# Expert rows added in DRAM to a residual row per token, in place of pair rows summed at the end

## The reference

```
ids = g_idx[..., None] * EXPERTS_PER_GROUP + e_idx
gates = jnp.sum(jax.nn.one_hot(ids, N_EXPERTS, dtype=f32) * e_w[..., None], axis=-2)
out = jnp.zeros(h.shape, f32)
for e in range(N_EXPERTS):
    y = (jax.nn.silu(h @ w_gate[e]) * (h @ w_up[e])) @ w_down[e]
    out = out + gates[..., e:e + 1] * y.astype(f32)
...
x = x + hier_moe(rmsnorm(x, norm2_g), ...)
y_prompt = rmsnorm(yp, final_norm_g)
```

## Time and profile before

| | us |
|---|---|
| median of 3 runs | 525.61 |
| lowest and highest | 524.95, 527.38 |
| profiled execution: its own time | 522.9 |
| profiled execution: span from the first instruction to the last | 521.1 |

### The profile page before, as it was taken

How to read it: one execution, slowest core, us unless ns; L and a number is a source line. 1 busy time by engine, 2 the same in 40 slices (tenths; PEclk the granted TensorE clock), 3 DMA queues, 4 the chain that set the end, 5 groups by cost and what they waited for, 6 DMA issues and landing times.

```text
span 521.1 us, 7055 instructions
## 1 busy us (share of the span) xinstructions
PE 468.7 (90%) x2479; PEld 368.4 (71%) x2479; DVE 335.5 (64%) x659; ACT 231.1 (44%) x446; POOL 106.3 (20%) x168
## 2 busy tenths in 40 slices
PE   6999899999999999999999887999999999999400
PEld 5879798877996777778887675776766776676100
DVE  4876515676585357766574687797478567765176
ACT  6664711563356447224132234556367366444021
POOL 5157001111000000001000333030322322312144
PEclk9999999999999999999999957999999999999955
DMA  8804404004008500610110967999899899800295
GB/s 304 191 12 164 170 0 162 0 1 162 1 1 220 160 13 2 181 42 0 42 62 1 346 259 299 419 413 374 340 364 380 353 356 376 336 28 25 71 333 187
DMA packets 33100, 93.15 MB, mean 179 GB/s; under 512 B 10248, under 2 KB 13456, under 8 KB 26928
## 3 DMA queue, kind: packets, MB, share of 16 engines
q1 hardware_dynamic: 27728, 82.81, 43.9%
q0 software_dynamic: 5344, 9.97, 5.3%
HBM read 88.38 MB, written 13.89 MB: 196 GB/s over the span
## 4 chain that ended last, share of the span: by engine, by line
PE 72%; DVE 11%; DMA 7%; ACT 4%; issue 3%; SPq 1%; POOL 1%; POOLq 0%; ACTq 0%; DVEq 0%
PE ps L2047 11%; PE ps L1724 7%; PE ps L1726 7%; PE ps L1725 7%; PE ps L2067 5%; PE ps L2069 5%; PE ps L2068 5%; PE ps L1936 3%; PE ps L1938 3%; PE ps L1937 3%; DMA pair<-y_pairs 2%; DMA h_rows<-s_buf 2%; PE ps L2028 2%; PE ps L1879 1%; PE ps L1876 1%
## 5 line engine op out<-in xcount | busy, mean ns | idle before, releaser
L1589 DVE TENSOR_TENSOR gu_lo<-we_gu,gu_hi 128x1024 fp32r<-128x1024 f32 x64 | 74.8, 1221 | 2.3 <-ACT gu_hi L1001 0.8
L1001 ACT ACTIVATE gu_hi<-we_gu 128x1024 fp32r<-128x1024 f32 x64 | 63.2, 1054 | 0.0
L2047 PE MATMUL ps<-we_d,hhT 128*128 128x512 f32 x128 | 56.9, 592 | 0.0
L2067 PE MATMUL ps<-gu_hi,xT_hi 128*128 128x512 f32 x128 | 52.9, 413 | 2.3 <-DVE xT_lo L1583 2.3
L2069 PE MATMUL ps<-gu_hi,xT_lo 128*128 128x512 f32 x128 | 50.7, 396 | 0.0
L2068 PE MATMUL ps<-gu_lo,xT_hi 128*128 128x512 f32 x128 | 50.6, 395 | 0.0
L1724 PE MATMUL ps<-hT_hi,w_hi 128*128 128x288 f32 x160 | 48.5, 303 | 1.6 <-DVE w_lo_q L1100 0.8
L2047 PEld LDWEIGHTS ps<-we_d,hhT 128*128 128x128 f32 x128 | 23.4, 191 | 24.9 <-issue 24.9
L1724 PE MATMUL ps<-w_hi,hT_hi 128*128 128x512 f32 x96 | 38.9, 406 | 0.3 <-DVE w_lo L1103 0.3
L1725 PE MATMUL ps<-w_lo,hT_hi 128*128 128x512 f32 x96 | 37.4, 390 | 0.0
L1046 ACT ACTIVATE sg<-ps 128x256 f32<-128x256 f32 x16 | 6.2, 385 | 62.6 <-PE ps L2069 57.4
(11 more groups left out here) (388 smaller groups left out, 1093.6 us busy)
## 6 DMA issues: line engine op xcount, KB each, us to landing
we_gu<-in_w_gate SPq DMA_DIRECT2D x16, 1024.0 KB, 8.1
we_gu<-in_w_up SPq DMA_DIRECT2D x16, 1024.0 KB, 13.7
we_d<-in_w_down SPq DMA_DIRECT2D x16, 1024.0 KB, 12.8
ring<-in_w_in SPq DMA_DIRECT2D x4, 2048.0 KB, 7.6
pair<-y_pairs SPq DMA_DIRECT2D x8, 512.0 KB, 7.7
ring<-in_w_in SPq DMA_DIRECT2D x3, 1024.0 KB, 8.2
x_first<-in_x_p SPq DMA_DIRECT2D x4, 512.0 KB, 9.8
x<-in_x_p SPq DMA_DIRECT2D x4, 512.0 KB, 3.8
```

The source lines that it names most:

```text
L1001: act.activation(gu_hi[slot % 2][:, :, 2 * q:2 * q + 2, :], we_gu[slot][:, :, 2 * q:2 * q + 2, :], ACT.Copy).then_inc(gu_hi_done, 1)
L1589: dve.tensor_tensor(gu_lo[slot][:, :, 2 * q:2 * q + 2, :], we_gu[slot][:, :, 2 * q:2 * q + 2, :], gu_hi[slot % 2][:, :, 2 * q:2 * q + 2, : ...
L2047: last = pe.matmul(bank(4 + 2 * (slot % 2) + half), hhT[:, slot % 2, f, :], we_d[slot][:, f, 512 * half:512 * half + 512], start=f == 0, s ...
L2067: pe.matmul(bank(0), xT_hi[:, c, :], gu_h[:, :, c, :], start=c == 0, stop=False)
```

## The change

`y_dram` with a row for each pair goes. In its place stands `sums_dram`, with a row for each token and 128 spare rows. `store_h2` stores the tile of x there, behind the tile of h2. The gates go to DRAM as well (`gates_dram`, one float for each pair), and POOL gathers them for each block into `slot_gate`, one per slot. `take_y` multiplies by this gate while it copies. POOL then adds the block's 128 rows to `sums_dram` with an indirect DMA that adds in place (`add_rows`); each waits for the one before it to have landed (`rows_added`). A third table, `table_dest`, names a slot's row in `sums_dram`; an unused slot gets the spare row of its partition, so all 128 rows are written. `weights` moves on DVE to a place ahead of the split of expert 1. In the tail SP loads five tiles in place of ten, `weigh` is gone, and ACT reads the sums as loaded.

```
@@ store_h2 (SP)
                 sp.dma_start(h2_dram[tok(t), :], h2[0:rows_of(t), t % 2, :]).then_inc(h2_stored[t], 16)
+                sp.dma_start(sums_dram[tok(t), :], x[0:rows_of(t), t, :]).then_inc(x2_stored, 16)
...
@@ SP, behind the loads of experts 2 and 3
             expert(3, 3, 2, 3)
+            sp.wait_ge(gates_ready, 1)
+            whole = gates_dram[0:2 * SEQ, :].rearrange("(t p i) o -> p t (i o)", p=P, i=2)
+            sp.dma_start(whole, gates[:, 0:PROMPT_TILES, :]).then_inc(gates_stored, 16)
...
+            sp.dma_start(rest, gates[0:DEC, PROMPT_TILES, :]).then_inc(gates_stored, 16)
...
@@ SP, tail
             for t in range(NT):
-                for i in range(2):
-                    cols = slice(i * D, (i + 1) * D)
-                    sp.dma_start(pair[0:rows_of(t), t, cols], pairs[tok(t), cols]).then_inc(pair_in[i][t], 16)
+                sp.dma_start(pair[0:rows_of(t), t, 0:D], sums_dram[tok(t), :]).then_inc(sums_in[t], 16)
...
@@ POOL
-            def scatter(slot, pairs):
...
+            def gather_gates(slot, pairs):
                 pool.indirect_dma_start(
+                    slot_gate[:, slot, :], None, gates_dram, bass.IndirectOffsetOnAxis(ap=pairs, axis=0),
+                    bounds_check=PAIRS - 1, oob_is_err=False).then_inc(gate_in[slot], 16)
+
+            def add_rows(slot, rows):
+                pool.indirect_dma_start(
+                    sums_dram, bass.IndirectOffsetOnAxis(ap=rows, axis=0), y[:, slot % 2, :], None,
+                    compute_op=ALU.add).then_inc(stored[slot % 2], 16)
+
+            def rows_added(i, slot):
+                if slot:
+                    pool.wait_ge(stored[(slot - 1) % 2], 16 * (2 * i + (slot - 1) // 2 + 2))
+                else:
+                    pool.wait_ge(stored[1], 16 * (2 * i + 1))
...
             gather(0, table_tok[:, AHEAD:AHEAD + 1])
+            pool.wait_ge(gates_stored, 32)
+            for s in range(UNROLL):
+                gather_gates(s, table[:, s:s + 1])
+            pool.wait_ge(x2_stored, 16 * NT)
...
                 pool.wait_ge(y_act, s + 3)
                 pool.wait_ge(y_dve, s + 3)
-                scatter(s, table[:, s:s + 1])
+                rows_added(0, s)
+                add_rows(s, table_dest[:, s:s + 1])
+                gather_gates(s, table[:, s + UNROLL:s + UNROLL + 1])
...
@@ take_y on ACT, and the same on DVE
+                act.wait_ge(gate_in[slot], 16 * (i + 1))
-                act.activation(y[:, slot % 2, 0:512], bank(4 + 2 * (slot % 2)), ACT.Copy).then_inc(y_act, 1)
+                act.activation(y[:, slot % 2, 0:512], bank(4 + 2 * (slot % 2)), ACT.Copy,
+                               scale=slot_gate[:, slot, :]).then_inc(y_act, 1)
...
@@ DVE
+            dve.tensor_scalar(table_dest[:, 0:NE], ps[:, 5, NE:2 * NE], float(NOWHERE // 2), spare_row,
+                              ALU.add, ALU.min)
...
             x_low(0, 1)
+            weights()
             gu_low(1, 1, 0, KC // 2)
...
-            def weigh(t):
-                r = rows_of(t)
-                for i in range(2):
-                    dve.wait_ge(pair_in[i][t], 16)
-                    dve.scalar_tensor_tensor(x[0:r, t, :], pair[0:r, t, i * D:(i + 1) * D], gates[0:r, i, t:t + 1],
-                                             x[0:r, t, :], ALU.mult, ALU.add).then_inc(sum_ready, 1)
...
-            weigh(0)
-            weigh(1)
-            for t in range(2, NT):
-                weigh(t)
-                final(t - 2)
-            final(NT - 2)
-            final(NT - 1)
+            for t in range(NT):
+                final(t)
```

More of the change, by code:

```diff
@@ L140, in program @@
         rk = place("rk", [P, NT, 2])
-        gates = place("gates", [P, 2, NT])
+        gates = place("gates", [P, NT, 2])
         rt = place("rt", [P, 12, NE])
@@ L145, in program @@
         table_tok = place("table_tok", [P, COLS], I32)
-        now_tok = place("now_tok", [P, UNROLL, 1], I32)
-        now_pair = place("now_pair", [P, UNROLL, 1], I32)
+        table_dest = place("table_dest", [P, COLS], I32)
+        now = place("now", [P, 3, UNROLL, 1], I32)
+        now_tok, now_pair, now_dest = (now[:, k, :, :] for k in range(3))
+        slot_gate = stats[:, 0:UNROLL, 6:7]
+        spare_row = stats[:, 0, 7:8]
         dec = place("dec", [P, BH, 2])
@@ L1061, in _ @@
                 r = rows_of(t)
-                act.wait_ge(sum_ready, 2 * t + 2)
-                act.activation(pair[0:r, t, D:2 * D], x[0:r, t, :], ACT.Square,
+                act.wait_ge(sums_in[t], 16)
+                act.activation(pair[0:r, t, D:2 * D], pair[0:r, t, 0:D], ACT.Square,
                                accum_out=stats[0:r, 2, t:t + 1]).then_inc(ssq3_ready, 1)
@@ L1513, in weights @@
                 chain(dve.tensor_tensor(sums, sums, halves, ALU.mult))
-                chain(dve.reciprocal(gates[:, 0, :], sums))
-                dve.tensor_tensor(gates[:, 1, :], gates[:, 0, :], rb[:, :, 4], ALU.mult).then_inc(gates_ready, 1)
+                chain(dve.reciprocal(gates[:, :, 0], sums))
+                dve.tensor_tensor(gates[:, :, 1], gates[:, :, 0], rb[:, :, 4], ALU.mult).then_inc(gates_ready, 1)
             over, incl, excl = (per_expert[:, a, :] for a in range(3))
@@ L1632, in group_of_blocks @@
                                     ).then_inc(hhT_ready, 1)
-                    if i is first and slot in (0, 3):
-                        (weights if slot == 0 else steering)()
+                    if i is first and slot == 3:
+                        steering()
                     if slot == UNROLL - 1:
```

46 lines of the change are left out of this document (26 added, 20 removed).

## The result

The changed kernel takes 542.4 us (median of 4 runs, 540.1 to 543.8) against 525.6 for the kernel before on the same chip: a ratio of 1.031, with a 95% interval of 1.028 to 1.035. It is slower, as forecast, but by 16.8 us and not by 8. The range (523 to 556) holds the time, and so does the forecast's own range (529 to 545).

The account below looks back on a forecast made before the run. PE was taken to set the pace, with the DMAs close behind. Tail -9, gates +3.5, ahead of the loop +2, last adds +3.5 and loop adds +8 gave +8: 531 us profiled, 534 median; range 523 to 556, forecast's own 529 to 545.

Parts of the forecast that it names:

- The tail: From the last landing to the last `final`: 16.2 us instead of 25.3, so 9 less (between 7 and 10).
- The first gates: Block 0's `take_y` newly waits for gates stored behind 6 MB of weights and then gathered: +3.5 us (bounds 0 and 8).
- The rival with the long wait: First gather of gates takes 13.6 us, 12.5 beyond cover, sum 543; chance 0.22 shared with dear adds, above 545.
- The adds in the loop: Block loop: adds of 128 rows and gathers of gates cost 3 us per group, 8 in all (between 0 and 38).
- by engine time: Count for the loop from DMA engine time per MB moved: 0 to 6 us a group, 0 to 16 in all.
- by pace: Count for the loop from 14 rows per us beside weights: 14 us more a group, 38 over 2.7 groups.
- the rival on dear adds: Loop: slow add landings set the pace; 15 us gives 569, 12 us gives 537; chance 0.22 shared with long gates, above 545.
- The last two adds: Blocks 14 and 15: the second add waits for the first's landing, 5 us each, +3.5 us (bounds 1 and 5).
- Ahead of the loop: Store of x before the last h2 store (1.4 us) and `weights` before the split (0.6): +2 us (between 1 and 3).
- The Trainium skill: Loop: a block's 128 rows are one turn per DMA engine, term near 1, not 8; gives the everything-hides rival, chance 0.13.

## Why the prediction was right, and where its sizes were off

**The tail** was worked out step by step from rows, as 16.2 us from the last landing to the last `final`. It measured 15.0 in the changed kernel and 15.2 when made alone; the first square began 3.6 us behind the landing and not 4.3. Between the same two points that is 10.3 less than before, just beyond the bounds of 7 and 10; the medians give 11.0 when made alone. The step that POOL's 128x1 operation lasts as long as DVE's beside it held (1.28 and 1.28).

**The first gates** were the term furthest off: +3.5 (0 to 8) against +7.8, confirmed by the run with the gates early (7.4). I had the gates' stores landing at 342; they landed at 340.6 and 346.2. I had given the first gather 4 us, by choice between 2.2 and 13.6; it took 5.5. I had 2 us of the wait covered, and 1.6 were: `y` of block 0 came 9.4 us late on top of the 4.6, `hh` of block 3 7.8. The rival with the long wait gave 543, close to the median, but by luck: its 12.5 us for this term (13.0 by its own numbers) is as far off on the other side, and it took its 13.6 us from a gather that waited behind others.

**The adds in the loop** came to +10.8 where I had +8. Of my two ways of counting, by engine time and by pace, neither is what decided. The count by engine time (0 to 16) had the term within its bounds, and reading is as dear as writing in it, as measured (0.328 us a row against 0.159). But it was the order that made PE wait, since without the order the 10.8 are gone though the engines do the same work. This is the rival on dear adds: 12 us a landing gives (12 - 10.4) x 11 less the 7 of lead, +11. The landings averaged 11.2, and 0.8 us passed from a landing to the next issue, which neither way counted. So the pace was 12.0, and a landing has to stay under some 9.6 us, not 10.4 (an estimate from these two numbers). That the rival's 11 is the measured term is partly luck: it takes off 7 us for the lead of the weights, but ACT waited for those by 0.6 us at most. What took up some 5 of the 16 us (1.6 for each of ten adds) were the two buffers of `y`, which put the first costly wait at block 7. I had priced that case at 537 because I let the other terms cancel; they came to +8.6.

**The last two adds**: +3.5 against +6.1. I took 5 us an add, with 5.4 as the bound from above, a gather and a scatter in a row. They took 5.98 and 5.89, and 0.8 us passed between them where I had 0.3. So that bound was too low: a row takes 0.33 us or more, and GpSimd takes 0.6 us longer to issue it.

**Ahead of the loop**: +2 against +4.6, of which 1.6 is the clock, and about +2 by the medians. The x store did cost 1.3 us at the last store of h rows, as worked out (1.4). The first store of h rows comes 0.44 us later than before. The expectation of the run with the late x stores puts that down to GpSimd's two constants ahead of `ident`, but `ident` is ready only 0.15 us later, PE's first operation no later, and the kernel with the skipped rows, which has the same constants, has that store where it was (226.8 against 226.7). The 0.44 has no shown cause.

**The Trainium skill**, "DMA: Bandwidth & Descriptors", on queues, rings and completion order, as the prediction applied it, would have made the loop's term about 1. The trace doesn't bear out that a block's rows are one turn of each engine: the adds land in 9.9 to 12.9 us beside weights and in 6 alone. Plain writes of the same rows land in 5.4 to 12.9.

The sum was +8 where +19.4 came, +17.8 without the clock. The direction and the parts were right, and the sizes were not. All four costs came out above the value I chose in the trace: the last two adds beyond their bound, the first gates 0.2 under theirs, what lies ahead of the loop at its bound once the clock is taken off. With PE busy throughout and the DMA engines full, little took them up. What I had put too low was a landing beside weights for the gates and the loop, and a landing alone for the last two adds.

## What to carry to other kernels

Adding in DRAM turned a sum at the end into a chain in the loop: as rows of two blocks may coincide, this kernel adds them one DMA after the other, and then the landing of an add, under load, and the time to the next issue have to be shorter together than the stage that feeds them. Compare that, and not the bytes, with the stage. A few KB (here 4.6, in pieces of 8 bytes) that somebody waits for are best not stored through the queue that holds megabytes of weights; issuing them on another queue gave back 7.4 us. When two waits are taken away together, look for the third resource behind them before adding up the gains. And before a stretch of two traces is compared, see whether the clock was the same in both.

## What the runs showed of the hardware

A packet of an adding DMA, a row of 4 KB, took 0.328 us (median), one of a plain write 0.159; with no weights beside them 128 rows landed in 5.9 to 6.3 us against 3.4. Its issue on GpSimd took 1.6 us, up to 2.4 beside other work, against 1.0.

Skipping slots by a bound on the index took away bytes but neither packets nor time: 8 packets of 4 KB stayed under way to the end in all three orders of the slots. Passing only 64 slots kept some 16 under way and did save time (4.7 us).

Beside weights, in the kernel where adds overlap, they landed in 10.1 to 12.6 us each, no later than adds one at a time (9.9 to 12.9).

A gather of 128 gates of 4 bytes that stood in the queue behind an add landed 0.2 to 0.7 us after that add: 4.1 to 4.7 us from its issue with no weights beside it, 8.6 to 11 beside them. Behind a plain write it took 2.3 to 3.3 us, with no weights beside it. With weights but no add in front it took 5.5 to 5.8 (the first four of the changed kernel).

PE's granted clock fell to the lower level (1.2 GHz) for a few microseconds in a stretch where PE was busy before and after. Every profiled execution but that of the kernel before had one or two such falls, near 237, 260 or 281 us; one cost 1.6 to 1.8 us, and that should be taken out before two traces are compared.
